# Output projection's weights cast on first load and written back in bf16, and the first feed-forward weights requested between the quarters of the first x tile

## The reference

```python
h = x
h = h + 0.5 * _swiglu(_rmsnorm(h, g1), wg1, wu1, wd1)          # ffn1
u = _rmsnorm(h, mix_norm)
z = u @ w_in                                                   # cq, ckv, krope, gq, gk, gv, ga, gr, xq, gz
o_mla, o_gla, o_x = attention, gated linear attention, cross-attention into 256 memory tokens
merged = gates[0] * o_mla + gates[1] * o_gla + gates[2] * o_x
h = h + merged @ w_out                                         # the output projection
h = h + 0.5 * _swiglu(_rmsnorm(h, g2), wg2, wu2, wd2)          # ffn2
out = _rmsnorm(h, final_norm)
```

## Time and profile before

| what | us |
|---|---|
| runs | 1883.79, 1625.87, 1625.35 (median 1625.87) |
| profiled execution, its own time | 1627.07 |
| its span, slowest core (core 2) | 1626.0 |
| spans of the eight cores | 1618.5 to 1626.0 |
| TensorE busy on core 2 | 1588.4 (98%) |

### The profile page before, as it was taken

How to read it: one execution, slowest core, us unless ns; L and a number is a source line. 1 busy time by engine, 2 the same in 40 slices (tenths; PEclk the granted TensorE clock), 3 DMA queues, 4 the chain that set the end, 5 groups by cost and what they waited for, 6 DMA issues and landing times.

```text
span 1626.0 us, 23823 instructions; the slowest of 8 cores (1618.5 to 1626.0 us)
## 1 busy us (share of the span) xinstructions
PE 1588.4 (98%) x7517; PEld 737.7 (45%) x7667; DVE 884.8 (54%) x1524; ACT 738.6 (45%) x1193; POOL 120.9 (7%) x227
## 2 busy tenths in 40 slices
PE   6999999999999999999999999999999999999997
PEld 2444444444444444444444444444444444444444
DVE  6666333557766466664565454476444445533347
ACT  5212211046765237882276874258587632311114
POOL 1101111100000000000000000000000000001000
PEclk9999999999999999999999999999999999999999
DMA  8779999997767455586787788587334344522212
GB/s 209 115 113 130 133 127 143 123 180 187 166 108 179 153 162 147 99 199 198 237 227 165 180 204 220 184 278 232 104 96 125 115 158 160 177 85 91 78 52 104
DMA packets 80712, 249.65 MB, mean 154 GB/s; under 512 B 9488, under 2 KB 13840, under 8 KB 80144
## 3 DMA queue, kind: packets, MB, share of 16 engines
q0 software_dynamic: 28720, 107.43, 38.3%
q1 hardware_dynamic: 51872, 140.70, 26.9%
HBM read 283.16 MB, written 54.26 MB: 208 GB/s over the span
## 4 chain that ended last, share of the span: by engine, by line
PE 94%; DMA 2%; DVE 1%; issue 1%; ACT 1%; POOL 0%; SPq 0%; DVEq 0%; ACTq 0%; POOLq 0%
PE ps_all L561 94%; DMA ring<-f1g 1%; DMA ring<-wb 1%; DVE hS L599 1%; DMA hS<-x 0%; ACT L587 0%; DVE mb L599 0%; ACT mb L587 0%; ACT ma L587 0%; DVE ntm L599 0%; PE ps_all L572 0%; DVE ma L594 0%; ACT fa L587 0%; DVE mb L611 0%; POOL ring L206 0%
## 5 line engine op out<-in xcount | busy, mean ns | idle before, releaser
L561 PE MATMUL ps_all<-ntm,ring 128*128 128x512 bf16 x2181 | 529.1, 379 | 3.6 <-ACT mb L587 0.6
L561 PE MATMUL ps_all<-B,ring 128*128 128x512 bf16 x1971 | 448.4, 379 | 2.7 <-DVE mb L594 0.2
L561 PEld LDWEIGHTS ps_all<-ntm,ring 128*128 128x128 bf16 x2224 | 217.1, 98 | 257.2 <-issue 4.3
L561 PEld LDWEIGHTS ps_all<-B,ring 128*128 128x128 bf16 x2016 | 196.6, 98 | 233.1 <-issue 1.1
L561 PE MATMUL ps_all<-aF,ring 128*128 128x512 bf16 (+1 forms) x1240 | 294.8, 374 | 4.9 <-DVE mb L599 3.1
L587 ACT ACTIVATE fa<-ps_all 128x512 f32<-128x512 f32 x170 | 101.3, 597 | 364.1 <-PE ps_all L561 351.8
L599 DVE SCALAR_TENSOR_TENSOR hS<-ps_all,hS 128x512 f32<-128x512 f32 (+1 forms) x256 | 170.1, 672 | 86.5 <-PE ps_all L561 85.4
L594 DVE TENSOR_TENSOR aF<-fa,ps_all 128x512 bf16<-128x512 f32 x151 | 103.2, 686 | 196.3 <-PE ps_all L561 186.1
L587 ACT ACTIVATE mb<-ps_all 128x512 bf16<-128x512 f32 (+1 forms) x304 | 165.5, 572 | 72.7 <-PE ps_all L561 70.6
L561 PEld LDWEIGHTS ps_all<-aF,ring 128*128 128x128 bf16 x1264 | 123.4, 98 | 143.6 <-issue 6.7
L587 ACT ACTIVATE ma<-ps_all,hv 128x512 f32<-128x512 f32 x104 | 71.1, 686 | 173.0 <-PE ps_all L561 164.9
(11 more groups left out here) (139 smaller groups left out, 1193.8 us busy)
## 6 DMA issues: line engine op xcount, KB each, us to landing
ring<-wb SPq DMA_DIRECT2D x112, 512.0 KB, 4.7
ring<-f1g POOLq DMA_DIRECT2D x44, 512.0 KB, 8.5
ring<-f2bg POOLq DMA_DIRECT2D x44, 512.0 KB, 3.9
wb<-wm POOLq DMA_DIRECT2D x28, 512.0 KB, 13.8
ma<-spill SPq DMA_DIRECT2D x48, 256.0 KB, 4.8
ring<-wb SPq DMA_DIRECT2D x48, 256.0 KB, 3.8
ring<-f2g POOLq DMA_DIRECT2D x22, 512.0 KB, 7.8
f2bg<-ring SPq DMA_DIRECT2D x22, 512.0 KB, 6.9
```

The source lines that it names most:

```text
L561: i = e.matmul(_ap(o), lhsT=_ap(l), rhs=_ap(r), start=st, stop=sp)
```

## The change

```diff
     def mload(name, i, k):
         b, n = MB[(name, i)]
         t = slot("rm")
-        f.dma("sp", t[:, 0:n], wb_T[b][:, 0:n], nbytes=128 * n * 2)
+        if wb_T[b].w is None:
+            f.dma("pool", t[:, 0:n], wm_d[b][:, 0:n], nbytes=128 * n * 4)
+            f.dma("sp", wb_T[b][:, 0:n], t[:, 0:n], nbytes=128 * n * 2)
+        else:
+            f.dma("sp", t[:, 0:n], wb_T[b][:, 0:n], nbytes=128 * n * 2)
         return t[:, 0:n].re("p (a b) -> p a b", a=k)
@@ load_x
             ops.append(op)
+            if t == 0 and c == 0:
+                f.dma("sp", vecs, vecs_d, nbytes=128 * NV * 4)
+            if t == 0 and c == 2:
+                early.append(wload(f1_d[0][0], 16))
         return ops
 
+    first, early = [], []
     x0 = load_x(0, 0)
-    f.dma("sp", vecs, vecs_d, nbytes=128 * NV * 4)
     x1 = load_x(1, 1)
     x2 = load_x(2, 2)
-    first = []
@@ ffn
         def load_gu(j):
-            wgu = wload(gu_d[j], 16, kind=ring_kind)
+            wgu = early.pop() if early else wload(gu_d[j], 16, kind=ring_kind)
@@ side1
-    todo = list(range(NMB))
+    todo = [b for (nm, i), (b, _) in MB.items() if not (nm in ('wout',) and i >= 0)]
-        for _ in range(3 if 14 <= j < 18 else 2 if j >= 3 else 0):
-            convert(todo.pop(0))
+        for _ in range(2 if j >= 3 else 0):
+            if todo:
+                convert(todo.pop(0))
@@ order of the opening
-    first[0].deps.add(x0[1].seq)
+    first[1].deps.add(x0[2].seq)
     for op in x1:
-        op.deps.add(first[0].seq)
+        op.deps.add(first[1].seq)
     for op in x2:
         op.deps.add(first[2].seq)
     first[3].deps.add(x1[2].seq)
```

## The result

| | before | after |
|---|---|---|
| median of 5 runs, us | 1625.87 | 1634.81 |
| ratio after / before | | 1.006, 95% interval 1.0048 to 1.0072 |
| span of the slowest core, profiled execution, us | 1626.0 (core 2) | 1634.5 (core 5) |
| span of the fastest core, us | 1618.5 | 1623.4 |
| HBM read, MB | 283.16 | 281.06 |

The change made the kernel 9 us slower by the medians and 9.7 by the ratio (interval 7.8 to 11.7 us). One of the five runs of before, 1883.79 us, had one die at a lower clock throughout, and the ratio leaves it out. The forecast was 1625.4 us, with a range up to 1630.5. It is not a matter of one unlucky core: the fastest core lost 4.9 us as well.

The account below looks back on a forecast made before the run. TensorE was taken as the bound, busy 1588.4 of 1626.0 us, leaving 37.6 us idle to win. Terms -0.5 - 0.3 + 0 + 0.3 = -0.5, taken with the runs' median of 1625.87, gave 1625.4 us, range 1619.5 to 1630.5.

Parts of the forecast that it names:

- two places with idle time to win ... and one where it can only lose: To win: the opening and perhaps the stall at 165 us; only to lose: 520 to 640 us, with tile 0's output projection.
- Part 1: Opening: weights 0 start earlier, but new waits for weights 1 and 2 give the early start back; -0.5 us.
- The bound of +2.6: Opening's upper bound: the fast core's 2.4 us wait lowers the clock (1.7 us) and tile 1's x comes a us late.
- Part 2: 42 conversions become 38, between 263 and 340 us, hidden behind TensorE; -0.3 us, bounds -0.8 and 0.
- Part 3: Stall at 165 us, where down weights come late: no edit touches it, scheduler order may alter; 0, bounds -3 and +3.
- rival B: Order at 165 us turns out luckier, 1622.9 us, or unluckier, 1629; chance 0.13.
- Part 4: Tile 0's output projection weights by four POOL cast loads and four SP write-backs; +0.3 us, bounds 0 and +3.
- cq lands some 4 us later, at 592 to 596, in time: Tile 1's cq loads, behind the write-backs on SP, arrive before its first projection, which can't start before 595.4 us.
- C: Opening: the wait for weights 1 costs clock, +2.6 us, 1628.5; chance 0.15 together with E.
- A: Opening: the early start stays, all 3 us kept because x and weights overlap better, 1622.9 us; chance 0.15.
- D: Output projection: only one of four slots circulates, so blocks follow each other; +47 us, 1673; chance 0.02.
- E: Opening: weights 0 still start at 9.4 us, only the later waits are left; +1.5 us; chance 0.15 together with C.

Follow-up runs that it names:

- e1: Kernel before with only the opening's edits; ratio 1.002 against before.
- e5: Kernel before, its issue order kept, with the opening's new waits and places for weights 0 to 2, tile 1's x and the norm gains; ratio 1.003.
- e7: As e5, but weights 1 wait for the second x quarter and tile 1's x for weights 0, as before; ratio 1.0033 against before.
- e11: Kernel before, order kept, with the two conversions issued at about 152 us on POOL moved behind that time's down weights (185 us, core 6); ratio 1.0033.
- e12: e11 plus wout cast loads as in e6, no write-backs, wout's conversions issued later (652 to 692 us, core 6); ratio 1.0026 against before.
- e14: As e12, but the conversion pair of 152 us goes near 324 us, behind the weight tile of 292 us; ratio 0.9987 against before.
- e2: Kernel before with only the wout part: 38 conversions, two a step, cast loads and write-backs in tile 0; ratio 1.0019 against before.
- e6: Kernel before, order kept, with wout's four cast loads and write-backs in tile 0 and their four conversions dropped; ratio 1.006.
- e10: Kernel after, its order kept, with tile 0's wout blocks loaded plainly by SP (gz blocks instead, output differs), no write-backs; ratio 1.0037 against before.
- e3: e2 without cast loads and write-backs; SP loads gz blocks in place of wout, so output differs; ratio 1.0089 against before.
- e4: e2 with the conversion pace of before (three a step for j = 14 to 17); ratio 1.0055 against before.
- e8: Kernel before with weights 0 to 2 waiting for the first x quarter instead of the second, norm gains after the first quarter; ratio 1.0006.
- e9: e6 without the four write-backs; later tiles load gz blocks in place of wout, so output differs; ratio 0.999 against before.

## Why the prediction was wrong, step by step

**"So the change touches two places with idle time to win ... and one where it can only lose."** The places were nearly right, the balance was not. The loss came at both the first and the last, and at one (340 to 430 us) that was not looked at.

**Part 1, the opening: wrong sign, 4 to 5 us off** (-0.5 forecast; e1 +3.3 by its ratio, interval 1.3 to 5.1; e5 +4.9, interval 2.9 to 6.8). The step that failed is "the second quarter and `vecs` are there by about 12". I had worked out when the sum of x and weights 0 would be through (15.7 us; the last quarter was there at 16.4), and taken from the old trace that the quarters before it would come evenly. They did not: the second came at 13.9, five us late. With it fell "step 0 is done about 3 us earlier": the first eight matmuls started 0.8 us before those of the earlier trace rows, and the third quarter's trigger came at 15.65 instead of 14.6. The second failure is one of omission: my only measure for tile 1 was its own x. The chain from tile 0's fourth quarter through its norm, the eight `B`, the silu and ScalarE's table load to tile 1's squares had little slack before (ScalarE waited 0.78 us for tile 1's x there, on core 2 at 26.41), and it starts 4 us later. That row also corrects the prediction's "13 us later": tile 1's x was there 10.1 us after its issue at 16.27, and its first matmuls came 3 us behind. The bound of +2.6 was built on the clock, which did not fall in the first 30 us of this core; the idle time alone was 3.4 us more there (12.24 to 15.62), and of another kind. Weights 1 were awaited at 22.3 for 0.72 us, where I had said 19 to 21: that step was nearly right, and e7 shows that it didn't matter.

The rule cited in the prediction, that DMA engines take turns between queues (the Trainium skill, DMA: Bandwidth & Descriptors, Queues, rings and completion order), speaks for what happened, and I had drawn too little from it: weights 0 delay each quarter behind the first, not only the sum. The fit that the Trainium skill gives for one DMA (same title, Anatomy of one DMA — SWDGE (gpsimd) path) had put all of them at 10.2 us, taken over the sum of their bytes. In this trace the last quarter came at 16.4 us.

**Part 2, fewer conversions: nothing, as bounded, but the reason given was too thin.** "They are hidden behind TensorE" is true. The prediction didn't ask which transfer stands behind them and how long it can wait. The tile of 290 us had 20.8 to 26.9 us between issue and landing before, and 15.6 to 19.3 after, without an idle microsecond of TensorE in either: the change did win some 5 us of landing time, and nobody was waiting for it. e11 and e12 show that the stretch can become critical: at 29 to 35 us TensorE waits 2 to 7.

**Part 3, the stall at 165 us: "value 0, bounds -3 and +3" held as a value.** It is there after as before on some cores (core 5 had 1.9 before and 3.1 after, now with a clock loss). Its cause, which the prediction only hinted at ("issued just behind conversions"), is shown by e11: take the pair away and it goes on all eight cores. What the prediction had wrong is the price: it would have booked 3 us for its removal (rival B). e11 shows that moved work comes back as a wait further down the same queue, and e14, where it doesn't, is 2.1 us faster than before (interval 0.5 to 3.7).

**Part 4, wout: +0.3 forecast, about +3 measured (e2), +10 at worst in another order (e6).** "cq lands some 4 us later, at 592 to 596, in time" is the step that failed physically. In e6 on core 0 the first two loads went out at 588 and 591 us, as computed, and landed 5.9 and 7.3 us later, not 4. The third went out at 595.7 and landed at 604.7, behind a second write-back that the prediction had not followed up to its slot. The row for a plain load in a quiet stretch (4.2 us) was applied to loads that share the engines with the writes. "No idle time over 1 us there" failed in the kernel after for another reason, the filler. The prediction counted the down matmuls as at hand "from 578.82 on the earlier trace rows". They were at hand because POOL had issued their weights by 507 us, and in the new order it didn't.

**What no part had: the order.** "The scheduler starts from other times, and its order there can alter" stood in one sentence, for one place, with a symmetric bound. It should have been a term of its own over the whole kernel. e10 and e3 put sizes to it: the wait at 591 us (2.0) is pure order, with 1.7 of clock behind it on six cores in after and on one in e10, and for the idle time between 340 and 430 us (up to 2.8) the order is enough, though e1, e7 and e11 show that a core which is late for another reason can get 1 to 4 us there in the order of before too. e2, e3 and e4, three small variants of the same part, came out at 1.0019, 1.0089 and 1.0055.

**The sum for core 5.** Idle time up to 975 us is 16.1 us before and 25.0 after, so 8.9 more. The two drops of the clock, 3.4 us long each at 1.2 GHz, cost 1.7 each: 3.4. That makes 12.3. The span grew by 11.7 us. Some 0.6 us the other way are not placed.

**Rivals.** C ("the wait for weights 1 costs clock", 1628.5) has the right sign and a fourth of the size, and its mechanism did not come in the kernel after. A clock loss in the opening did come in e5 and e7, behind another wait. A and D did not come: no early start was kept, and four slots circulated. B did not either: at 165 us some cores stall and others do not, on both sides. E is excluded by the row of 1.57 us and the HBM figure. The range failed because its upper end was C alone with a margin. The bounds that I had written for the parts, +2.6, 0, +3 and +3, add to 8.6, which gives 1625.9 + 8.6 = 1634.5. That this meets the measured 1634.8 is luck: of the four bounds only those of the opening and of wout were used up, and 2.8 us stood where no part had looked.

## What to carry to other kernels

When a load is let go earlier beside others that all feed one chain, ask of each of them, not of the last one, when it lands; and follow the chain behind the last one as far as the next tile. A transfer saved is worth something only if it stands in the queue ahead of something that is waited for: read the landing time of the tile behind it, not the share of busy engines. Where a scheduler or planner sets the order, an edit of its input is a new draw for everything behind it (e2, e3 and e4 spread over 0.7%): hold the order fixed to see what the edit costs, and give the draw a term of its own in a forecast.

## What the runs showed of the hardware that I had not expected

- A second DMA queue with one 1 MB cast load on it does not slow the four x quarters evenly. Over the eight cores of after, e5 and e7 the first came at 5.9 to 8.1 us, against 5.8 to 7.3 before, and the second at 11.1 to 14.7 against 8.7 to 9.6. With the load issued behind the first quarter, at 6.3 to 7.6 us (e8), the first was there at 5.8 to 7.1 and the second at 9.0 to 10.0.
- A wait of 1.99 us of TensorE, with the same work before and behind, was followed by 3.4 us at the lower level of the clock (1.2 GHz) on six cores of after and by none on two; in e10 by it on one core and by none on seven. The prediction had taken 1.90 us as harmless from one core.
- A weight tile on POOL's queue can take 21 to 27 us from issue to landing while TensorE stands still nowhere for it (before); at 29 to 35 us it waited 2 to 7 (e11, e12). Two conversions moved from 152 to 185 us, out of a time when the queue would otherwise have been empty, put the tile off by 9 us.
- Write-backs of 512 KB from SBUF to HBM took 6.2 to 10.3 us to land on core 0 of e6, and the four plain loads issued between and behind them 5.9 to 10.8, where such a load had taken 4.2. The cast loads of the same blocks took 6.4 to 12.6 us there. Without the write-backs (e9) the cast loads cost nothing.
